# Expert weights in 2 MB matrices with 16 KB runs, and TensorE taking a team's experts in pairs

## The reference

```python
g_prob = softmax(xt @ w_rg + b_rg);  p_grp, grp = top_k(g_prob, 1)        # 4 groups of 8 experts
top_p, top_i = top_k(softmax(e_in), 2)                                    # 2 experts in the group
...
hid = silu(xb @ w_gate[e]) * (xb @ w_up[e])      # w_gate, w_up: 1024 x 512
y   = (hid @ w_down[e]) * w                      # w_down: 512 x 1024
out = zeros.at[token].add(y)
```

## Time and profile before

| | us |
|---|---|
| median of 3 runs | 1640.85 (1640.3 to 1641.03) |
| the profiled execution, its own time | 1641.66 |
| its span | 1639.9 |
| TensorE matmul busy | 1311.4 (80%) |
| VectorE busy | 739.9 (45%) |
| ScalarE busy | 291.8 (18%) |
| DMA, mean over the span | 210 GB/s |
| expert stage, first expert matmul to the end of the scatter | 1160.83 to 1625.82 |

### The profile page before, as it was taken

The page is one execution under the profiler, slowest core; times in us unless marked ns, Lnnn a source line. Parts: engine busy times, 40 slices in busy tenths (PEclk is TensorE's granted clock), DMA queues, the critical chain, the costliest instruction groups (busy, mean ns, idle before and its releaser), DMA issues. The chain is left out here.

```text
span 1639.9 us, 18015 instructions
## 1 busy us (share of the span) xinstructions
PE 1311.4 (80%) x7207; PEld 950.9 (58%) x7207; DVE 739.9 (45%) x1105; ACT 291.8 (18%) x405; POOL 65.8 (4%) x138
## 2 busy tenths in 40 slices
PE   0957879999799979999799979996676676577574
PEld 0823449999688668999678767574333233133131
DVE  1989775877414558777201666133220220121122
ACT  1002033333222523342102210121000000000000
POOL 1135200000000000000000000000000000000000
PEclk9967889999899989999999799997888888888787
DMA  5600734465434326465544134431599999999994
GB/s 152 135 4 1 256 103 154 157 218 164 154 124 124 113 78 205 156 214 169 160 128 154 52 110 147 132 125 64 235 422 422 422 421 422 422 422 422 422 422 180
DMA packets 144381, 343.77 MB, mean 210 GB/s; under 512 B 17202, under 2 KB 106412, under 8 KB 119748
## 3 DMA queue, kind: packets, MB, share of 16 engines
q1 hardware_dynamic: 136392, 338.18, 55.5%
q0 software_dynamic: 1504, 4.47, 1.5%
q10 hardware_dynamic: 6428, 0.33, 0.3%
HBM read 340.33 MB, written 2.62 MB: 209 GB/s over the span
## 5 line engine op out<-in xcount | busy, mean ns | idle before, releaser
L916 PE MATMUL ps<-HT_hi,piece_hi 128*128 128x256 f32 x704 | 199.1, 283 | 7.8 <-DVE HT_lo L1473 7.8
L1309 PE MATMUL ps<-ring,arena 128*32 128x512 f32 x1024 | 142.6, 714 | 78.3 <-DMA ring<-in_w_exp_up_dram 77.0
L917 PE MATMUL ps<-HT_lo,piece_hi 128*128 128x256 f32 x704 | 199.4, 283 | 0.0
L918 PE MATMUL ps<-HT_hi,piece_lo 128*128 128x256 f32 x704 | 199.3, 283 | 0.0
L864 PE MATMUL ps<-HT,ring 128*128 128x256 f32 x832 | 187.8, 388 | 8.4 <-ACT HT L613 5.4
L864 PEld LDWEIGHTS ps<-HT,ring 128*128 128x128 f32 x832 | 160.6, 194 | 34.8 <-issue 7.4
L1482 DVE TENSOR_TENSOR piece_lo<-ring,piece_hi 128x2048 fp32r<-128x2048 f32 x66 | 148.5, 2288 | 38.5 <-ACT piece_hi L654 38.5
L654 ACT ACTIVATE piece_hi<-ring 128x2048 fp32r<-128x2048 f32 x66 | 123.8, 1916 | 136.2 <-PE ps L918 136.2
L1309 PEld LDWEIGHTS ps<-ring,arena 128*32 128x32 f32 x1024 | 38.6, 129 | 176.5 <-issue 176.5
L916 PEld LDWEIGHTS ps<-HT_hi,piece_hi 128*128 128x128 f32 x704 | 134.9, 192 | 9.4 <-DVE HT_lo L1473 8.6
L917 PEld LDWEIGHTS ps<-HT_lo,piece_hi 128*128 128x128 f32 x704 | 134.9, 192 | 0.8
(11 more groups left out here) (365 smaller groups left out, 1567.8 us busy)
## 6 DMA issues: line engine op xcount, KB each, us to landing
ring<-in_w_exp_gate_dram SPq DMA_DIRECT2D x64, 1024.0 KB, 19.2
ring<-in_w_exp_up_dram SPq DMA_DIRECT2D x64, 1024.0 KB, 15.7
ring<-in_w_exp_down_dram SPq DMA_DIRECT2D x64, 1024.0 KB, 16.2
ring<-in_ffn_w_gate_dram SPq DMA_DIRECT2D x22, 1024.0 KB, 6.2
ring<-in_ffn_w_up_dram SPq DMA_DIRECT2D x22, 1024.0 KB, 5.4
ring<-in_ffn_w_down_dram SPq DMA_DIRECT2D x22, 1024.0 KB, 7.3
ring<-in_w_in_dram SPq DMA_DIRECT2D x20, 1024.0 KB, 5.5
ring<-in_odd_w_in_dram SPq DMA_DIRECT2D x12, 1024.0 KB, 5.5
```

The costliest lines, as they stand in the source:

```text
L916: pe.matmul(out, sh, mh, start=start, stop=False, skip_group_check=True)
L917: pe.matmul(out, sh, ml, start=False, stop=False, skip_group_check=True)
L918: return pe.matmul(out, sl, mh, start=False, stop=stop, skip_group_check=True)
L1309: ins = pe.matmul(ps[own, 2 + up, :], mGT[:, kt, own], w[e][:, k4, :], start=(kt == 0), stop=(kt == KT - 1))
```

## The change

The same bytes go through the same ring in the same 48 blocks, but a load is now a whole matrix of 2 MB. It fills two neighbouring slots, and each partition's part is one run of 16 KB in DRAM and in SBUF. It waits until both slots are free, and one semaphore, that of the first slot, stands for both. A team has 12 loads in place of 24.

A block of 4 MB now holds the whole matrices of two experts in place of half matrices of four. TensorE therefore takes the experts in two pairs: for gate, up and down alike first experts 0 and 1 with all rows, then experts 2 and 3. The number of matmuls, their shapes, and the points at which `piece_used` goes up by 4 stay. The hidden values' transposes take every fourth column, so that the rows of down that a partition holds (4p to 4p+3) meet the right hidden values.

```diff
+PAIRS = [(0, 1), (2, 3)]
...
-                        sp.wait_ge(piece_used, g * TEAM_PIECES + (k - RING + 1))
-                        dst = ring[:, k % RING, :].rearrange("p (k c) -> p k c", k=src.shape[1])
-                        sp.dma_start(dst, src).then_inc(loaded[k % RING], 16)
-                        k += 1
+                        sp.wait_ge(piece_used, g * TEAM_PIECES + (k - RING + 2))
+                        dst = ring[:, k % RING:k % RING + 2, :].rearrange("p a b -> p (a b)")
+                        sp.dma_start(dst, src.rearrange("(p k) n -> p (k n)", p=P)).then_inc(loaded[k % RING], 16)
+                        k += 2
                     for w in (wg, wu):
-                        for half in range(2):
-                            for e in range(TEAM):
-                                put(w[bass.ds(it * (TEAM * D) + e * D, D), :]
-                                    .rearrange("(p k) n -> p k n", p=P)[:, KT // 2 * half:KT // 2 * (half + 1), :])
-                    for half in range(2):
                         for e in range(TEAM):
-                            put(wd[bass.ds(it * (TEAM * D_EXPERT) + e * D_EXPERT + half * UNIT, UNIT), :]
-                                .rearrange("(p k) n -> p k n", p=P))
+                            put(w[bass.ds(it * (TEAM * D) + e * D, D), :])
+                    for e in range(TEAM):
+                        put(wd[bass.ds(it * (TEAM * D_EXPERT) + e * D_EXPERT, D_EXPERT), :])
...
-                    w = ring[:, k % RING, :].rearrange("p (k c) -> p k c", k=n)
-                    k += 1
-                    return w
+                    w = ring[:, k % RING:k % RING + 2, :].rearrange("p a b -> p (a b)")
+                    k += 2
+                    return w.rearrange("p (k c) -> p k c", k=n)
...
-                    for half in range(2):
-                        w = [take(KT // 2) for e in range(TEAM)]
-                        for k4 in range(KT // 2):
-                            kt = KT // 2 * half + k4
-                            for e in range(TEAM):
+                    for pair in PAIRS:
+                        w = {e: take(KT) for e in pair}
+                        for kt in range(KT):
+                            for e in pair:
                                 own = slice(e * SLOTS, (e + 1) * SLOTS)
-                                ins = pe.matmul(ps[own, 2 + up, :], mGT[:, kt, own], w[e][:, k4, :],
+                                ins = pe.matmul(ps[own, 2 + up, :], mGT[:, kt, own], w[e][:, kt, :],
                                                 start=(kt == 0), stop=(kt == KT - 1))
                                 pay(ins)
-                        if half == 0:
+                        if pair == PAIRS[0]:
                             ins.then_inc(piece_used, TEAM)
...
-                    for half in range(2):
-                        for f in range(2):
-                            ins = pe.transpose(ps[:, 7, (2 * half + f) * P:(2 * half + f + 1) * P],
-                                               mH[:, half * UNIT + f:(half + 1) * UNIT:2], ident[:, :])
+                    for f in range(4):
+                        ins = pe.transpose(ps[:, 7, f * P:(f + 1) * P], mH[:, f::4], ident[:, :])
...
-                def down(half):
-                    w = [take(2) for e in range(TEAM)]
-                    for f in range(2):
+                def down(pair):
+                    w = {e: take(4) for e in pair}
+                    for f in range(4):
                         for c in range(2):
-                            for e in range(TEAM):
+                            for e in pair:
                                 own = slice(e * SLOTS, (e + 1) * SLOTS)
-                                ins = pe.matmul(ps[own, 4 + c, :], mHT[:, 2 * half + f, own],
-                                                w[e][:, f, c * 512:(c + 1) * 512], start=(half == f == 0),
-                                                stop=(half == f == 1))
+                                ins = pe.matmul(ps[own, 4 + c, :], mHT[:, f, own],
+                                                w[e][:, f, c * 512:(c + 1) * 512], start=(f == 0), stop=(f == 3))
                                 pay(ins)
-                    ins.then_inc(m_y_full if half else piece_used, 1 if half else TEAM)
+                    last = pair == PAIRS[1]
+                    ins.then_inc(m_y_full if last else piece_used, 1 if last else TEAM)
```

More of the change, by code:

```diff
@@ L1346, in team @@
                 pe.wait_ge(m_ht, g + 1)
-                down(0)
-                down(1)
+                down(PAIRS[0])
+                down(PAIRS[1])
                 owed = True
```

## The result

| | before | changed |
|---|---|---|
| median, us | 1641.32 (1638.76 to 1643.51, 20 runs) | 1643.49 (1640.55 to 1650.04, 20 runs) |
| ratio to before | | 1.0016, 95% interval 1.0008 to 1.0023 |
| the profiled execution, its own time | 1641.66 | 1641.71 |
| its span | 1639.9 | 1640.0 |
| TensorE matmul busy | 1311.4 (80%) | 1406.8 (86%) |

The forecast was 0.7 us less than before and 1640.1. The medians say 2.2 us more, a small slowdown about as large as the bound for "no change"; 1643.49 lies within the range. (A ratio here is not the quotient of the two medians; the two can differ a little.) The changed kernel also scatters more: its slowest run lies 9.5 us above its fastest, where before that was 4.8. The profiled execution is one of the quicker ones, 1.8 us under its median, and shows less than the whole loss.

The account below looks back on a forecast made before the run. The expert stage was taken as bound by weight transfers at 422 GB/s. Terms -6.4 (rate), +3.4 (first block), +2.3 (last block) and nothing for TensorE's pace gave -0.7 us, 1640.1 us; range 1636.0 to 1647.0.

Parts of the forecast that it names:

- bound for "no change": Whole kernel: 0.2%, 3.3 us, about what a measurement can tell from no change; chance of "same" 0.57.
- Term 1, the transfer rate: Expert weight stream: 16 KB runs cut a block from 9.94 to 9.80 us, 6.4 us less over 45 blocks.
- the line through the 1 KB and 8 KB rows: DMA packet cost fitted from two run sizes: 37.8 ns per KB and 9.1 ns fixed, giving 6.4 us less.
- The rows of 2 KB (3.2 ns) and of 1 KB with 2 KB (13.5 ns): Other fixed packet costs: 2 KB with 8 KB saves 2.3 us (rival, 14%); 1 KB with 2 KB 9.7 (rival, 13%).
- The bound of nothing: Weight stream: 16 KB runs may be cut into 8 KB packets and save 0; rival at 1646.6, 14%.
- Term 2, the first block: Stage start: first block takes 6.83 us instead of 3.42, so transfers start 3.4 us later.
- Term 3, the last block: Stage end: last block takes 7.7 us instead of 5.34, 2.3 us later, bounds 1.5 and 3.2.
- Term 4, TensorE's pace: Expert teams: TensorE goes from 70% to 94% of the beat, still gives blocks back in time; costed at nothing.
- margin of 2.4 us: Behind a team's last down block: transfers run dry after 22.6 us, block back after 18.7, request needs about 1.5.
- The rival of 5%, late refills in a mild form: Expert teams: refills late by up to 2 us a team, up to 14 us more; 5%.
- waits of 25 to 35 us: TensorE in the expert stage: waits for weights should fall from 142.6 us to some 25 to 35.
- Slices below 418 with DMA under 1.0: Sign in the expert stage's 41 us slices, in GB/s: TensorE gives blocks back too late.

Follow-up runs that it names:

- e7: Changed kernel (16 KB runs, pairs) with most expert matmuls left out, all weights still loaded: 1632.09 us, ratio 0.9942.
- e6: Kernel before (8 KB runs, experts side by side) with most expert matmuls left out, all weights still loaded: 1637.71 us, ratio 0.9976.
- e3: Changed kernel with the next team's gather moved from behind the last down block to before the hidden values' transposes: 1641.1 us, ratio 1.0001.
- e9: Changed kernel with 8 identity transposes, about 1 us, ahead of each team's second up pair and second down pair: 1641.98 us, ratio 1.001.
- e4: Changed kernel with 16 more identity transposes behind each gather: 1651.86 us, ratio 1.0052.
- e10: Changed kernel with every team's gate and the last team's down in 1 MB pieces, four experts side by side: 1637.93 us, ratio 0.998.
- e8: e3 with the first team's gate and the last team's down in 1 MB pieces, four experts side by side: 1638.7 us, ratio 0.9983.

## Why the prediction was right in its parts and wrong in its sum

**Term 1, the transfer rate: right.** Forecast -6.4 us, measured -6.7 (e7 against e6) to -7.0 (against the kernel before). Over 45 blocks, 16 engines and 16 packets fewer per engine and block that is 6.69 / 45 / 16 = 9.3 ns to 9.7 ns for each packet saved, where the line through the 1 KB and 8 KB rows said 9.1. The number of DMAs halved as well: two small completion packets of some 10 ns each fall away per engine and block. They are in these figures; without them it is about 8 ns. No run here tells the price of a DMA from that of a packet any further. The rows of 2 KB (3.2 ns) and of 1 KB with 2 KB (13.5 ns) were too short to lean on. The bound of nothing fell with the packet count. The Trainium skill, page "DMA: Bandwidth & Descriptors", section "Why small descriptors are slow (HBM only)", gives 3 cycles per packet, an estimated 3.5 ns. The line through the 2 KB and 8 KB rows was near it, the stream of e7 is not, and the longer measurement decides.

**Term 2, the first block: right.** Forecast 3.4, measured 3.40.

**Term 3, the last block: right within its bounds.** Forecast 2.3 as half of a low start, bounds 1.5 and 3.2, so no single outcome was named; it was 7.06 us, 1.72 more than the 5.34 before, in all six kernels with all matmuls whose last block was a pair. The low start did not come behind the waits of 2.69 us (changed kernel) and 2.70 us (e3) there, though it did behind such waits at other places.

**Term 4, TensorE's pace: wrong, and it decided the sign.** The failed step is "I cost it at nothing", on a margin of 2.4 us "into which one low start (1.7 us) fits". The rival of 5%, late refills in a mild form, is what happened. The first half of the step held: the request came 1404.98 - 1386.42 = 18.6 us after the end of the last down block, where 18.7 was forecast. The other half was how long the transfers last, and there the forecast allowed too much, for two reasons:

- A block starts some 0.6 us after its weights have landed. Worked out from the trace's DMA records, the last landing of the stage is at 1613.64 and the block starts at 1614.26. The forecast counted the transfers' reserve from the block's start, so the reserve was 0.6 less.
- The 16 engines don't run dry together. In the records of 1228 to 1235 us the leading engine completes its share of a load 5.49 us after the one before, the slowest still in 4.88: the request of 1226.37 was late for the first and in time for the last. From there the spread between them is 1.4 us in place of 2.0. A first late refill costs only that lead. But the lead does not come back, because the slowest engine falls behind again by itself: near 1597 to 1604 its loads take 5.37 and 5.42 us, 4.89 being regular, though they had been asked for 7.5 us ahead and more, while the leading engine keeps its 4.89. e7, where no refill is late, shows the same near 1210. So in the end the stream pays nearly what the leading engine was late: 0.8 us in e9, 2.7 in e3 and 12.6 in e4, where their streams were 0.9, 2.6 and 11.8 us over e7's.

With those the margin is 1.8 us for the slowest engine and about nothing for the leading one. One low start (1.4 us at 1377.96) takes most of what is left, which is what the rows at 1378 to 1409 show.

The low start is not needed for a late refill, though. Counted on the leading engine, the loads behind the requests of 1226.37, 1285.10, 1344.80 and 1404.98 came 0.60, 0.76, 0.27 and 1.37 us late, 3.0 in all, and only the last of the four had a long down block in front of it. The other three down blocks took 7.06 us and had still waited for their weights, so nothing ahead of them had made them late. The request of 1285.10 cost the slowest engine 1.1 us, more than any other. The down block in front of it, the request and two windows behind it:

```profile
1259.52 7.06 PE L1324 MATMUL ps<-ring,arena 128*32 128x512 f32 x32 [1.19 <-DMA ring<-in_w_exp_down_dram]
...
1285.10 0.83 SPq L431 DMA_DIRECT2D ring<-in_w_exp_up_dram  x2
...
1286.00:1288.00 2.00, 2.00 (x12) 0.54 (x10) 0.00 (x0) 0.00 (x0) 0.00 (x0) 1.00 0.98 369
1288.00:1290.00 2.00, 2.00 (x18) 0.75 (x16) 0.00 (x0) 0.00 (x0) 0.00 (x0) 1.00 0.98 344
```

The engines are counted busy there (share 0.98) but move only 369 and 344 GB/s: the records hold two dozen packets of 0.7 to 1.9 us in place of 0.61. Packets of that length stand behind the requests of 1226.37 and 1404.98 too. What slows them no run here shows.

Put together for the profiled execution: 0.46 less before the stage, +3.40, -4.59 (the 7.0 less 2.4 of late refills), +1.72, which is +0.1, as its span shows. For the medians: 3.4 + 1.7 - 7.0 = -1.9 where +2.2 was measured, so about 4 us of late refills in a typical run. That last figure is a difference and was not seen in a trace; e3, which got 2.3 us of it back, e4 (8.5 more) and e10 (late refills gone, the sum as worked out) speak for it.

**What would show it.** Right: slices of 427 and more, 9.8 us between blocks, the packets, the first refill. Not right: waits of 25 to 35 us were 40.8, and matmul time of 328 with some low starts was 322.5, because neighbouring blocks overlap (below). "Slices below 418 with DMA under 1.0" was the right sign for late refills, but set too low: a refill late by 1 us takes only 2% from a slice of 41 us, and slices of 418 to 422 among ones of 429 were already the sign.

Open stay: which waits are followed by a low start and which not (2.7 us was, at 1377.96, and was not, at 1614.26; 0.98 us was, at 1428.66), why packets behind a late request were slow, and what makes the slowest DMA engine fall behind near 1600. A packet of 16 KB on the instruction queue falls there (1597.41), but the kernel before and e10 have one as well, at 1599.35 and 1594.99, without such a step. Open is also why e6 and e8 reached the stage late.

## What to carry to other kernels

When a ring feeds an engine, work out the margin between "slots given back" and "transfers run dry" from the landing and not from the engine's start, for the leading DMA engine as well as the last, and treat a margin of 1 to 2 us as none: here it was used up with and without a change of clock, and the scatter of the runs (9.5 us in place of 4.8) showed it. Longer runs need not be bought for all transfers: keeping the blocks small and wide at the places where an end or a refill hangs on them (first, last, and behind the long stretch of other work), and large elsewhere, kept 4.4 of the stream's 7.0 us here and gave back only 0.8 at the last block. And to price a rate alone, compare the stretch from the first refill to the last block, not whole times.

## What was not expected of the hardware

- Blocks of pairs that follow each other without a wait overlap. Three blocks took 17.43 to 17.99 us, where three of 6.83 are 20.5: the next pair's matmuls, on other column tiles, start beside the last ones of the pair before. From 1165.55 on the trace has four records a round in place of two, 1.9 us before the first block's last record ends. The first block alone was not shortened (7.09 us to the refill).
- Behind an idle 2.7 us TensorE sometimes starts at 1.2 GHz (0.50 over 1378 to 1380), once also behind 0.98 us (1428.70 to 1430.70), and the block takes 1.3 to 1.7 us more; with 1 us of useless transposes in the gap no block behind a filled gap of e9's profile was long.
- From 8 to 16 KB a packet saved, with its share of the completion packets, is still worth 9.3 to 9.7 ns: nearly the 9.1 of the line that 1 KB and 8 KB packets gave.
- In a full stream the slowest of the 16 DMA engines completes a load some 2.0 us behind the leading one, and a late request is paid by the leading one first.
